# Seven-product projections in the scan of both layers, decays scaled on GpSimd, token sums kept

## The chip, the cores and the metric

The kernel runs on one core of one Trainium2 chip. Its time is the device time of one execution in microseconds. It is one launch that computes both blocks of the reference.

## The reference, cut to what matters

The first block is an attention block with a feed-forward part. The second block has two layers on 512 tokens: 256 latent tokens and 256 context tokens. The change sits in its layers, in the part that prepares and runs the state-space scan:

```python
def ssd_inputs(xbc_raw, dtf_raw, dtb_raw, conv_w, conv_b, dt_bias_f, dt_bias_b):
    xbc = dwconv_silu(xbc_raw, conv_w, conv_b)          # 5 taps along the tokens, then silu
    xs, bm, cm = jnp.split(xbc, [...], axis=-1)         # x 2048 wide, B and C 8 groups x 128
    ...
# ssd_chunked, chunks of 128 tokens, forward and backward
xc = x * dt
cs = cumsum(dt * a)
chunk_states = einsum('bclgn,bclgr,bclgrp->bcgrpn', bc, exp(cs[:, :, -1:] - cs), xc)
lmat = exp(where(lower, seg, -inf))                     # seg: differences of cs inside a chunk
y = einsum('bclsg,bclsgr,bcsgrp->bclgrp', cb, lmat, xc) + einsum(..., cc, h_in, exp(cs))
# ssd_output
rmsnorm((yf + yb + ssd_d * xs) * silu(z), ssd_norm_g) @ w_ssd_o
```

`xbc_raw`, `z`, the time steps and the attention inputs are all slices of one product, `h @ w_in`, with `h` 512 tokens x 1024 in fp32. Layer 0 returns both token sets. Layer 1 returns the latent tokens only, so C and z are needed for 256 tokens there and x and B for 512.

## The kernel before

All activations stay in SBUF, features on the partitions and tokens along the free dimension. Weights come as tiles of 1024 x 128 (512 KB) through a ring of 10 slots, `W`, in the order of a list (`weight_tiles`). SyncE issues each load when its slot is free. The engines run from orders that are written out by hand, with semaphores between them.

**The scan.** It runs over 8 groups `g`. A group has six projection tiles: x0, x1, B, C, z0, z1. `front(g, t)` on TensorE makes one, as 8 matmuls over the contraction, each 512 tokens wide in layer 0; the trace shows an fp32 matmul as two instructions. The tiles of group g+1 are made between the steps of group g. TensorE's group is: `turned` (transposes of B, the C by B products, transposes of x), the states of three steps, the outputs of the chunks (4 in layer 0, 2 in layer 1), and the tiles of g+1 in between. Each raw tile lies in a PSUM bank. ScalarE's `center` multiplies it by the middle tap into `xs`, VectorE's `conv` adds the other four taps (L2409, `in0` from PSUM), ScalarE's `activated` applies silu.

**The decays.** GpSimd broadcasts the rows of cumulated sums from DRAM (`broadcast`). ScalarE computes differences and exponentials into `mt` (`below`, `raised`). VectorE's `masked` multiplies each of 8 128x128 blocks of a chunk by its time step and by the masked C by B product (L2445), and adds both directions (L2449). `decayed` makes the scaled x (L2422), `carried` the carried state (L2434, L2438). GpSimd multiplies the exponentials `ec` by C (L754: 6 instructions per group in layer 0, 4 in layer 1) and adds up squares for the norm (L765, two per group).

**Seven products.** Later stages (merge0, wout20, f10, f20, all in layer 0) already use a form with seven products for two tiles: with the contraction halved, the two output tiles and the two token halves, eight block products become seven. One such *unit* is `quick(j)`: 7 times 4 matmuls of 256 tokens into the banks A, D, C, B. GpSimd makes four weight sums of 128x512 (L781, L783, L784, L786), into two further slots of the ring. VectorE makes the token sums (`tokens_summed`, four instructions of 128x1024, or three when the same tokens are summed again). ScalarE copies the first part out of PSUM (`first_kept`), and VectorE's `combined` makes the results from it with five more instructions, one input always in PSUM (256, 256, 512, 256 and 512 columns, L2610 to L2624).

## Time and profile before

| what | value |
|---|---|
| median of 3 runs | 2700.45 us (2700.17 to 2704.59) |
| the profiled execution, its own time | 2700.33 us |
| its span | 2698.5 us |
| TensorE busy | 2669.2 us (99%) |
| VectorE busy | 1292.7 us (48%) |
| ScalarE busy | 761.9 us (28%) |
| GpSimd busy | 622.5 us (23%) |

The span goes from the first to the last instruction of the profiled execution; 1.8 us of its time lie around it. Shares are means over stages with different limits, so the rows below are taken stage by stage. Every row of a timeline gives the start, the duration, the engine and the line of the code; rows of one line that follow each other without a gap are merged, with their number behind the x.

### The profile page before, as it was taken

Reading aid. Unit: us, or ns where it says so; the run is one execution under the profiler, and the core shown is the slowest. Engines: PE = TensorE matmul, PEld = TensorE weight load, DVE = VectorE, ACT = ScalarE, POOL = GpSimd, SP = SyncE. Lnnn points to the kernel's source line nnn. Section 1 sums busy time; section 2 is a strip of 40 time slices with the busy share of each in tenths; the row PEclk is TensorE's granted clock in tenths of the full one; section 3 lists DMA queues with packets and bytes.
Section 4 is the critical chain, followed back from the end, with each engine's and each line's share of the span. In section 5 each row is a group of like instructions: output and inputs, shape, how many; then the busy total and the mean of one; then the engine's idle time right before and its main releaser. Section 6 shows DMA issues by size and latency. Waiting matters only on the chain.

```text
span 2698.5 us, 33892 instructions
## 1 busy us (share of the span) xinstructions
PE 2669.2 (99%) x13090; PEld 1984.5 (74%) x13090; DVE 1292.7 (48%) x2279; ACT 761.9 (28%) x1740; POOL 622.5 (23%) x534
## 2 busy tenths in 40 slices
PE   8999999999999999999999999999999999999999
PEld 6778885555555666788778888866666777888887
DVE  1432234778778334787668451146677523212101
ACT  2430002656656333100022110015545422101100
POOL 4000000223323122275424454403122122000000
PEclk9999999999999999999999999999999999999999
DMA  9356666434342221233355432264344222567552
GB/s 264 96 160 194 187 194 171 106 103 110 91 111 66 55 55 39 63 110 103 100 160 184 142 92 87 86 168 126 104 115 111 79 71 65 155 188 210 153 151 78
DMA packets 518992, 330.62 MB, mean 123 GB/s; under 512 B 15296, under 2 KB 485680, under 8 KB 518832
## 3 DMA queue, kind: packets, MB, share of 16 engines
q1 hardware_dynamic: 507600, 296.10, 38.7%
q0 software_dynamic: 10784, 31.46, 4.7%
q8 instruction: 105, 1.72, 0.3%
q10 hardware_dynamic: 448, 0.89, 0.1%
q14 instruction: 55, 0.45, 0.1%
HBM read 327.06 MB, written 1.34 MB: 122 GB/s over the span
## 4 chain that ended last, share of the span: by engine, by line
PE 93%; DVE 2%; issue 2%; ACT 1%; PEld 1%; POOL 0%; DMA 0%; DVEq 0%; PEldq 0%; POOLq 0%; ACTq 0%
PE ps L1266 43%; PE ps L1646 23%; PE ps L1802 4%; PE ps L1814 3%; PE ps L1793 3%; PE ps L1955 3%; PE ps L1777 2%; PE ps L1916 1%; PE ps L1754 1%; PE ps L1939 1%; PE ps L1587 1%; PE ps L1928 1%; PE ps L2032 1%; PE ps L1292 0%; PE ps L1740 0%
## 5 line engine op out<-in xcount | busy, mean ns | idle before, releaser
L1266 PE MATMUL ps<-xnT,W 128*128 128x256 f32 (+1 forms) x2912 | 901.3, 468 | 2.2 <-DVE TMP L2409 0.9
L1266 PEld LDWEIGHTS ps<-xnT,W 128*128 128x128 f32 x2912 | 549.6, 190 | 320.0 <-issue 257.9
L1266 PE MATMUL ps<-BIG,W 128*128 128x256 f32 x1440 | 315.0, 379 | 0.0
L1266 PEld LDWEIGHTS ps<-BIG,W 128*128 128x128 f32 x1440 | 272.6, 190 | 37.1 <-issue 0.4
L1646 PE MATMUL ps<-TMP,W 128*128 128x256 f32 x1192 | 273.3, 379 | 0.0
L1646 PEld LDWEIGHTS ps<-TMP,W 128*128 128x128 f32 x1192 | 226.5, 190 | 30.8
L1646 PE MATMUL ps<-BIG,W 128*128 128x256 f32 x1016 | 230.5, 379 | 0.0
L803 ACT ACTIVATE TMP<-ps 128x512 f32<-128x512 f32 (+5 forms) x172 | 89.5, 528 | 440.9 <-PE ps L1646 209.6
L1646 PEld LDWEIGHTS ps<-BIG,W 128*128 128x128 f32 x1016 | 192.8, 190 | 27.1 <-issue 1.0
L2409 DVE SCALAR_TENSOR_TENSOR TMP<-ps,prmT,TMP 128x510 f32<-128x510 f32 (+3 forms) x256 | 181.6, 714 | 42.6 <-ACT TMP L1002 27.8
L2445 DVE SCALAR_TENSOR_TENSOR TMP<-TMP 128x128 f32<-128x128 f32 x384 | 162.4, 494 | 41.6 <-ACT TMP L1038 41.6
L1646 PE MATMUL ps<-xnT,W 128*128 128x256 f32 x704 | 161.0, 380 | 0.0
L781 POOL TENSOR_TENSOR W<-W 128x512 f32<-128x512 f32 x52 | 72.6, 1396 | 366.7 <-PE ps L1646 224.6
L754 POOL TENSOR_TENSOR BIG<-BIG,TMP 128x512 f32<-128x512 f32 x80 | 104.0, 1315 | 227.2 <-ACT BIG L1044 227.2
L1646 PEld LDWEIGHTS ps<-xnT,W 128*128 128x128 f32 x704 | 133.4, 190 | 18.6 <-DVE TMP L2624 0.4
L2140 DVE SCALAR_TENSOR_TENSOR TMP<-W,cact,TMP 128x512 f32<-128x512 f32 x168 | 142.4, 882 | 8.0
L730 POOL TENSOR_TENSOR TMP<-TMP,cst 32x512 f32<-32x512 f32 x56 | 71.6, 1279 | 274.6 <-ACT TMP L803 272.1
L1814 PE MATMUL ps<-W,xnT 128*128 128x128 f32 x1024 | 123.0, 276 | 0.0
L1814 PEld LDWEIGHTS ps<-W,xnT 128*128 128x128 f32 x1024 | 118.2, 192 | 3.8 <-issue 3.8
L1802 PE MATMUL ps<-xnT,W 128*128 128x512 f32 x256 | 119.0, 599 | 0.0
L832 ACT ACTIVATE xnT<-hT 128x512 f32<-128x512 f32 (+1 forms) x48 | 24.7, 522 | 333.8 <-DVE hT L2366 154.4
L1028 ACT ACTIVATE TMP<-BIG,TMP 128x128 f32<-128x128 f32 x384 | 116.8, 389 | 1.5 <-PE ps L1777 1.5
(350 smaller groups left out, 3002.5 us busy)
## 6 DMA issues: line engine op xcount, KB each, us to landing
W<-in_w_in SPq DMA_DIRECT2D x188, 512.0 KB, 4.0
W<-in_w_mlp SPq DMA_DIRECT2D x128, 512.0 KB, 4.0
W<-in_ada_w SPq DMA_DIRECT2D x96, 512.0 KB, 4.0
BIG<-cs_rows POOLq DMA_DIRECT2D x96, 256.0 KB, 4.7
W<-in_w_ssd_o SPq DMA_DIRECT2D x32, 512.0 KB, 3.6
W<-in_w_gate SPq DMA_DIRECT2D x22, 512.0 KB, 5.1
W<-in_w_up SPq DMA_DIRECT2D x22, 512.0 KB, 3.9
W<-in_w_down SPq DMA_DIRECT2D x16, 512.0 KB, 3.8
```

The costliest lines, as they stand in the source:

```text
L754: nc.gpsimd.tensor_tensor(e, e, xs[:, 3, ch * P:(ch + 1) * P].unsqueeze(1) .to_broadcast([P, 4, P]), ALU.mult).then_inc(ssd["ec"], 1)
L803: return A(dst, src, ACT.Copy)
L1028: last = A(mt[:, (2 * c + d) % 4, h, :], csb[:, ch, d, h, :], ACT.Relu, scale=-1.0, bias=tabs[:, 2, ch, span(g * 4 + 32 * d + h, 1)])
L1266: last = mm(dst, w[:, c, 0:m], rhs(k), start=k == 0, stop=k == total - 1)
L1646: done = mm(PS[bank][:, half * S:half * S + S], w[:, at + c, :], x[:, c, :], start=first and opens and c == 0, stop=last and closes and c ...
L1793: last = mm(PS[bq][:, 0:nt], w[:, c, :], xnT[:, c, 0:nt], start=c == 0, stop=c == KC - 1)
L1802: last = mm(PS[bk][:, :], w[:, c, :], xnT[:, c, :], start=c == 0, stop=c == KC - 1)
L1814: last = mm(PS[bq if h else 5][:, t * P:(t + 1) * P], xnT[:, c, t * P:(t + 1) * P], w[:, c, :], start=c == 0, stop=c == KC - 1)
L1955: last = mm(PS[4 + 2 * (i % 2) + n][:, 0:nt], w[:, c, :], xn(c), start=c == 0, stop=c == KC - 1)
L2140: last = V.scalar_tensor_tensor(out=dst, in0=w[:, k, :], scalar=c, in1=dst, op0=ALU.mult, op1=ALU.add)
L2409: last = V.scalar_tensor_tensor(out=acc[:, :, lo:hi], in0=raw[:, :, lo + k - 2:hi + k - 2], scalar=tap(l, g, t, k), in1=acc[:, :, lo:hi], ...
L2445: V.scalar_tensor_tensor(out=mt[:, c % 4, h, :], in0=mt[:, c % 4, h, :], scalar=tabs[:, 0, order[i], span(g * 4 + 32 * d + h, 1)], in1=cbm ...
```

## The change

- **Scan projections as units.** In layer 0 each group's (x0, x1), (B, C) and (z0, z1) become units of seven products, 24 in all. In layer 1 only (x0, x1) do, 8 in all. All use the banks 0, 1, 4, 5, so each unit waits, bank by bank, for `combined` of the unit before it. Their weight sums go to GpSimd inside the scan, and take two ring slots each.
- **Raw tiles in SBUF.** `combined` puts the raw tiles into `yz` or `zs`; `center`, `conv` and `gated` read them there and not in PSUM.
- **Decays.** GpSimd's `by_dt` multiplies `mt` by the time steps (one 128x512 instruction per chunk and direction). VectorE's `masked` becomes one instruction of 128x1024 and one of 128x512.
- **Scaled x.** VectorE copies all transposed x out of PSUM first (`xc`), and `decayed` reads that copy in SBUF.
- **Kept token sums.** The sums of the normed tokens get a place of their own (`TX`), are made once at the start of each scan and of f10, and serve the gate units of merge0 as well.
- **Order.** The time-step tile goes first in each scan, then the x unit. In layer 0, `masked(g, 1)` stands ahead of the convolutions, `masked(g, 2)` behind the first two, and two decay steps of the next group are moved up on ScalarE. One broadcast per chunk takes the place of two. The scratch for DMA descriptors is 8192.

```diff
+PARTS = {"x0": ("x0", "x1"), "bc0": ("B", "C"), "z0": ("z0", "z1"), "x1": ("x0", "x1")}
+QUICK = [(x, g, 0) for g in range(NG) for x in ("x0", "bc0", "z0")]
...
+    ph, n, _ = QUICK[FIRST_OF[g]]
+    if ph in PARTS:
+        return [0, 1, 4, 5]
...
+                def weights_summed(j):
+
+                    *pair, k1, k2 = quick_keys(j)
+                    wa, wb, w1, w2 = (slot_of(key) for key in (*pair, k1, k2))
+                    for key in pair:
+                        pool.wait_ge(slot_full[number[key] % SLOTS], full_at[number[key]])
+                    for key in (k1, k2):
+                        pool.wait_ge(slot_used[number[key] % SLOTS], number[key] // SLOTS)
+                    nc.gpsimd.tensor_tensor(w1[:, 0:4, :], wb[:, 0:4, :], wb[:, 4:8, :], ALU.add)
+                    pool.drain()
+                    nc.gpsimd.tensor_tensor(wb[:, 0:4, :], wa[:, 0:4, :], wb[:, 0:4, :], ALU.subtract)
+                    nc.gpsimd.tensor_tensor(w1[:, 4:8, :], w1[:, 0:4, :], wa[:, 0:4, :], ALU.subtract)
+                    pool.drain()
+                    nc.gpsimd.tensor_tensor(w2[:, 0:4, :], wa[:, 4:8, :], w1[:, 4:8, :], ALU.subtract).then_inc(q_s, 1)
+
+                def by_dt(g, i):
+
+                    ch = order[i]
                     for d in range(2):
-                        pool.dma_start(csb[:, ch, d, :, :], bass.AP(
-                            tensor=cs_dram, offset=(g * 4 + 32 * d) * T + ch * P, ap=[[0, P], [T, 4], [1, P]]))\
-                            .then_inc(csb_in[ch], 16)
-
+                        c = 2 * (n_ch * g + i) + d
+                        R("mexp", c + 1)
+                        m = mt[:, c % 4, :, :]
+                        nc.gpsimd.tensor_tensor(m, m, tabs[:, 0, ch, span(g * 4 + 32 * d, 4)].unsqueeze(2)
+                                                .to_broadcast([P, 4, P]), ALU.mult).then_inc(ssd["mdt"], 1)
+
...
                 for g in range(NG):
                     for i, ch in enumerate(order):
+                        by_dt(g, i)
...
                         if g < NG - 1:
                             broadcast(g + 1, i)
+                        if l == 0 and i == 1 and g < NG - 1:
+                            weights_summed(unit("bc0", g + 1))
+                            weights_summed(unit("z0", g + 1))
+                    if g < NG - 2:
+                        weights_summed(unit(f"x{l}", g + 2))
...
                 def center(g, t):
-                    made(act, ("ssd", l, g, FRONT[t]))
+                    if not is_quick(l, t):
+                        made(act, ("ssd", l, g, FRONT[t]))
                     if g:
                         R("tr", 3 * g)
                         if t < 2:
@@ -999,7 +1080,8 @@
                         if t == 3:
                             R("ec", len(parts) * g)
                     n = wide_of(t)
...
+                    if l == 0:
+                        if g == 0:
+                            decays(0, 0)
+                            below(0, 1)
+                        raised(g, 1)
...
+                if ph in PARTS:
+                    pe.wait_ge(dt_dve, 9 * int(ph[-1]) + 1)
+                    pe.wait_ge(ssd["xc"], ssd_first["xc"] * int(ph[-1]) + n)
...
+                def front(g, t):
+                    if t < 4:
+                        pe.wait_ge(q_rel, 3 * quick_group(unit("x1", g)) + 1)
+                    else:
...
-                front(0, 0, shifted("f20" if l else "down1"))
+                ready = shifted("f20" if l else "down1")
...
-                front(0, 2)
+                quick(unit(f"x{l}", 0))
+                if l == 0:
+                    after = quick_steps(unit("bc0", 0))
+                    for _ in range(3):
+                        next(after)
+                else:
+                    front(0, 2)
                 pe.wait_ge(dt_dve, 9 * l + 3)
...
-                        front(g + 1, 0)
+                        x_unit = quick_steps(unit(f"x{l}", g + 1))
+                        for _ in range(4):
+                            next(x_unit)
...
+                    if more and l == 0:
+                        quick(unit("bc0", g + 1))
...
-                    raw = PS[t % 2][:, 0:n].rearrange("p (s n) -> p s n", n=S)
+                    raw = (kept_tile(l, g, t) if is_quick(l, t) else PS[t % 2][:, 0:n]).rearrange("p (s n) -> p s n", n=S)
...
-                                               PS[4 + ch // 2][:, (ch % 2) * S:(ch % 2) * S + S]
-                                               .rearrange("p (h e) -> p h e", e=HD), per_head(1, ch, d, g), ALU.mult)
+                                               xc[:, ch, :].rearrange("p (h e) -> p h e", e=HD),
+                                               per_head(1, ch, d, g), ALU.mult)
...
                 def masked(g, i):
-                    for d in range(2):
-                        c = 2 * (n_ch * g + i) + d
-                        R("mexp", c + 1)
-                        for h in range(4):
-                            V.scalar_tensor_tensor(out=mt[:, c % 4, h, :], in0=mt[:, c % 4, h, :],
-                                                   scalar=tabs[:, 0, order[i], span(g * 4 + 32 * d + h, 1)],
-                                                   in1=cbm[:, d, order[i], :], op0=ALU.mult, op1=ALU.mult)
-                    dve.drain()
-                    V.tensor_tensor(mt[:, (c - 1) % 4, :, :], mt[:, (c - 1) % 4, :, :], mt[:, c % 4, :, :], ALU.add)\
-                        .then_inc(ssd["mready"], 1)
+                    c = 2 * (n_ch * g + i)
+                    m = mt[:, c % 4:c % 4 + 2, :, :]
+                    R("mdt", c + 2)
+                    V.tensor_tensor(m, m, cbm[:, :, order[i], :].unsqueeze(2).to_broadcast([P, 2, 4, P]), ALU.mult)
+                    dve.drain()
+                    V.tensor_tensor(m[:, 0, :, :], m[:, 0, :, :], m[:, 1, :, :], ALU.add).then_inc(ssd["mready"], 1)
...
-                conv(0, 0)
+                dve.wait_ge(n_sh, 8 * NORMS["f20" if l else "down1"])
+                all_summed(sums_job(unit(f"x{l}", 0)))
...
                 adds(*GAP["f20" if l else "down1"])
+                combined(unit(f"x{l}", 0))
+                conv(0, 0)
                 conv(0, 1)
-                conv(0, 2)
+                if l == 0:
+                    combined(unit("bc0", 0))
+                else:
...
-                    R("tr", 3 * g + 2)
+                    R("tr", 3 * g + 3)
+                    if g:
+                        R("ychunk", n_ch * g)
+                    for b in range(2):
+                        last = V.tensor_copy(flat(xc[:, 2 * b:2 * b + 2, :]), PS[4 + b][:, :])
+                    last.then_inc(ssd["xc"], 1)
                     dve.drain()
                     cb = PS[7][:, 0:nt].rearrange("p (c t) -> p c t", t=P)
                     for d, tri in enumerate((upper, lower)):
                         last = V.tensor_tensor(cbm[:, d, 0:n_ch, :], cb, tri.unsqueeze(1).to_broadcast([P, n_ch, P]), ALU.mult)
                     last.then_inc(ssd["cbm"], 1)
-                    R("tr", 3 * g + 3)
                     if g:
                         R("states", 3 * g)
                     decayed(g, 0)
                     decayed(g, 1)
-                    if g:
-                        R("ychunk", n_ch * g)
-                    for b in range(n_ch // 2):
-                        last = V.tensor_copy(flat(xc[:, 2 * b:2 * b + 2, :]), PS[4 + b][:, :])
-                    last.then_inc(ssd["xc"], 1)
                     R("cbm", g + 1)
                     masked(g, 0)
                     carried(g, 0)
                     decayed(g, 2)
+                    if l == 0:
+                        masked(g, 1)
                     if more:
+                        combined(unit(f"x{l}", g + 1))
+                    dve.drain()
+                    carried(g, 1)
+                    if l and more:
+                        masked(g, 1)
                         conv(g + 1, 0)
-                    elif l == 0:
+                    dve.drain()
+                    carried(g, 2)
+                    if l and not more:
                         masked(g, 1)
-                    dve.drain()
-                    carried(g, 1)
                     if more:
-                        masked(g, 1)
+                        if l == 0:
+                            conv(g + 1, 0)
                         conv(g + 1, 1)
-                    dve.drain()
-                    carried(g, 2)
                     if l == 0:
                         masked(g, 2)
+                        if more:
+                            combined(unit("bc0", g + 1))
                         masked(g, 3)
-                    elif not more:
-                        masked(g, 1)
                     if more:
...
+                    if more and l == 0:
+                        combined(unit("z0", g + 1))
```
## Rows read from the trace of the kernel before

**Rows 1.** Page, parts 1 and 4: busy time by engine, and the chain by engine.

```profile
PE 2669.2 (99%) x13090; PEld 1984.5 (74%) x13090; DVE 1292.7 (48%) x2279; ACT 761.9 (28%) x1740; POOL 622.5 (23%) x534
...
PE 93%; DVE 2%; issue 2%; ACT 1%; PEld 1%; POOL 0%; DMA 0%; DVEq 0%; PEldq 0%; POOLq 0%; ACTq 0%
```

**Rows 2.** Windows: one group of layer 0, one of layer 1, then the two openings.

```profile
core 0: us, PE busy (x) PEld busy (x) DVE busy (x) ACT busy (x) POOL busy (x), PEclk, DMA share, GB/s
...
627.53:678.88 51.35, 51.33 (x210) 26.76 (x209) 38.59 (x73) 32.32 (x67) 16.32 (x16) 1.00 0.39 103
...
1908.77:1947.15 38.38, 38.38 (x173) 24.61 (x172) 26.71 (x54) 19.72 (x43) 9.45 (x10) 1.00 0.41 110
423.60:473.93 50.33, 50.06 (x180) 24.75 (x177) 26.96 (x51) 16.27 (x32) 6.51 (x9) 1.00 0.64 165
1791.21:1832.00 40.79, 39.91 (x178) 24.49 (x175) 25.98 (x52) 15.28 (x31) 3.58 (x5) 1.00 0.62 161
```

**Rows 3.** Timeline, TensorE, layer 0 (start, us): transposes of two groups, one pair of tiles.

```profile
576.18 0.60 PE L1729 MATMUL ps<-cst,TMP 128*128 128x128 f32 x4
...
603.96 13.90 PE L1266 MATMUL ps<-xnT,W 128*128 128x512 f32 x32
...
627.53 0.60 PE L1729 MATMUL ps<-cst,TMP 128*128 128x128 f32 x4
```

**Rows 4.** Timeline, TensorE, stage f10: one seven-product unit and the start of the next.

```profile
1443.39 3.62 PE L1646 MATMUL ps<-TMP,W 128*128 128x256 f32 x16
...
1455.47 3.62 PE L1646 MATMUL ps<-TMP,W 128*128 128x256 f32 x16
```

**Rows 5.** Timeline, VectorE, layer 0, two groups of the scan.

```profile
604.16 0.76 DVE L2434 TENSOR_TENSOR TMP<-TMP 128x256 f32<-128x256 f32 x2 [2.58 <-PE ps L1754]
...
611.63 4.21 DVE L2445 SCALAR_TENSOR_TENSOR TMP<-TMP 128x128 f32<-128x128 f32 x8
...
616.52 6.33 DVE L2409 SCALAR_TENSOR_TENSOR TMP<-ps,prmT,TMP 128x508 f32<-128x508 f32 x8
...
624.11 1.29 DVE L2562 TENSOR_TENSOR BIG<-BIG 128x512 f32<-128x512 f32 x2
...
646.86 2.19 DVE L2445 SCALAR_TENSOR_TENSOR TMP<-TMP 128x128 f32<-128x128 f32 x8
```

**Rows 6.** Timeline, GpSimd, same stretch.

```profile
612.23 2.67 POOL L754 TENSOR_TENSOR BIG<-BIG,TMP 128x512 f32<-128x512 f32 x2 [0.23 <-ACT BIG L1044]
```

**Rows 7.** Timeline, GpSimd and VectorE side by side, stage merge0.

```profile
1299.87 1.22 DVE L2577 TENSOR_TENSOR TMP<-BIG,TMP 128x1024 f32<-128x1024 f32 x1
...
1303.75 1.27 POOL L783 TENSOR_TENSOR W<-W 128x512 f32<-128x512 f32 x1
...
1304.98 2.25 POOL L784 TENSOR_TENSOR W<-W 128x512 f32<-128x512 f32 x1
1306.19 2.11 DVE L2575 TENSOR_TENSOR TMP<-BIG,TMP 128x1024 f32<-128x1024 f32 x1
...
1307.37 2.06 POOL L786 TENSOR_TENSOR W<-W 128x512 f32<-128x512 f32 x1
1308.23 2.29 DVE L2577 TENSOR_TENSOR TMP<-BIG,TMP 128x1024 f32<-128x1024 f32 x1
```

**Rows 8.** One line each: ns shortest/median/longest; carried state, last part of a unit, GpSimd over hT.

```profile
L2434 DVE TENSOR_TENSOR TMP<-TMP x64: 418/424/1483, 489.4 to 2115.0; 128x256 f32<-128x256 f32 x64
...
L2624 DVE TENSOR_TENSOR TMP<-TMP,ps x32: 686/687/689, 1152.4 to 1782.7; 128x512 f32<-128x512 f32 x32
...
L795 POOL TENSOR_TENSOR hT<-hT,prmT x1: 3603/3603/3603, 1170.0 to 1170.0; 128x2048 f32<-128x2048 f32 x1
```

**Rows 9.** Timeline, VectorE, first and last step of the time-step chain, layer 0.

```profile
434.63 0.47 DVE L2469 TENSOR_SCALAR BIG<-ps,small 128x256 f32<-128x256 f32 x1
...
444.46 0.35 DVE L2493 TENSOR_SCALAR BIG<-BIG,small 128x256 f32<-128x256 f32 x1
```

**Rows 10.** Windows, TensorE clock just ahead of stage f10.

```profile
1378.00:1388.00 10.00, 9.77 (x59) 5.33 (x62) 3.54 (x9) 1.92 (x4) 0.00 (x0) 0.83 0.99 299
```

428 lines of the change are left out of this document (246 added, 182 removed).

## The prediction

> **What bounds the kernel now.** I read the page first: TensorE is busy 99% of the span, and 93% of the chain that ended last is TensorE [rows 1]. VectorE and GpSimd look half empty, but those are means over the whole span. So I went on to the windows of the stretches that the change touches. One group of layer 0's scan takes 51.35 us, with TensorE busy all of it and VectorE for 38.6; one of layer 1 takes 38.38 us, VectorE 26.7 [rows 2]. The starts of two `turned` give the same 51.35 us [rows 3]. The reader is to see that TensorE sets the scan today, and that VectorE has only 12.8 us a group to spare in layer 0. Then I read VectorE and GpSimd side by side, since the change loads both.
>
> **What TensorE saves.** A pair of 512-wide tiles takes 13.90 us in 32 instructions [rows 3]. A unit takes 12.08 us (1455.47 - 1443.39) [rows 4]: 1.8 us less. Three units a group leave TensorE 51.35 - 3 x 1.8 = 45.95 us in layer 0, and one leaves 38.38 - 1.8 = 36.6 us in layer 1. With 32 units, 58 us would go if TensorE stayed the bound everywhere.
>
> **What VectorE and GpSimd do to each other.** Near 1305 us both work on SBUF alone. A VectorE instruction of 1024 columns takes 1.22 us by itself and 2.11 and 2.29 us beside GpSimd; a GpSimd one of 512 columns takes 1.27 us by itself and 2.25 and 2.06 beside VectorE [rows 7]. They take turns. The carried state, 256 columns, takes 0.42 us, but 1.48 once [rows 8]. Eight of L2445 take 2.19 us alone and 4.21 us while two of GpSimd run (2.67 us) [rows 5, 6]: nearly the sum. A part of a unit with one input in PSUM never waits: shortest 686 ns, longest 689 [rows 8]. So each time a GpSimd instruction meets a VectorE one with two SBUF inputs, VectorE loses 2.11 - 1.22 = 0.89 to 1.07 us for a full one; I take 0.85, since `by_dt` is shorter (below).
>
> The Trainium skill says the same in "SBUF — State Buffer", section "Who interferes with whom": the pair of ports is an exclusive lock, held for the whole instruction, and a VectorE instruction with two SBUF inputs contends with a GpSimd one that reads SBUF. The trace agrees on who contends, but its price is 0.2 to 0.4 us under a whole instruction of 1.27. By the skill's wording the group of layer 0 would last at least the sum of both engines' such instructions, 33.6 + 25.2 = 58.8 us as an estimate, and the kernel 2752 us.
>
> **What the change puts on that path, layer 0, one group.** GpSimd: 12 weight sums, 6 `ec`, 2 sums of squares at 1.27 us, and 8 `by_dt`. For `by_dt` the nearest row has its broadcast along the inner axis as well: 3.60 us for 2048 columns [rows 8], so about 1.0 us for 512; 1.27 is the other end. Sum 20 x 1.27 + 8 x 1.03 = 33.6 us, before 8 instructions and 16.3 us with the broadcasts [rows 2]. One broadcast takes the place of two per chunk, which gives GpSimd back 3 us of issue; it lies beside other work.
>
> VectorE: the copies of x 1.28 and the masked products 1.28 (pairs of 512 columns, as [rows 5]); `decayed` 6 x 0.33 = 2.0; `masked` 4 x (1.22 + 0.08 + 0.61) = 7.7, before 4 x (2.2 to 4.2, + 0.7); carried state 0.6 + 2 x 1.45 = 3.5; the convolutions 16 x 0.80 = 12.9 (616.52: 6.33 for 8); three `combined` at 2.7 = 8.1, from 0.69 and 0.41 us rows and their gaps; the gated output 2.55. Sum 39.3 us. So `masked` gives back what `combined` costs. That is without meetings. What is new is where inputs lie: `conv` (16) and `decayed` (6) read PSUM before and SBUF now. With `masked` (8), `carried` (4) and the output (2), 36 instructions can meet GpSimd's 28.
>
> How many do? I followed both orders by hand from the last transpose of a group. GpSimd's two sums of squares run under VectorE's PSUM copies, two or so under each of `combined` x and `combined` bc, and one or two under the carried additions. GpSimd then waits for the squares of the next group, so it can't spread its work. That leaves 19 meetings: 16.2 us. VectorE then needs 39.3 + 16.2 + 1.1 (waiting for the last transposes, since those wait for z's `combined`) = 56.6 us. A second way to the same number: the third `masked` ends after 22.9 us of VectorE's own work and 17 meetings, at 37.4 us; `outputs(g, 2)` on TensorE waits for it, from about 30 us on, when bc is done; behind it are queued the z unit and the next group's `turned`: 1.5 + 6.9 + 1.4 + 5.2 + 0.7 + 0.9 = 16.6, in all 54.0 us. VectorE's own order is the later one. I take 56.6 us, 5.25 more than now. Seven groups (the last projects nothing): +36.8 us. Break-even is 51.35, or 13 meetings.
>
> **Layer 1.** GpSimd gets 4 `by_dt` and 4 weight sums, VectorE 27.5 us of own work, with convolutions of x alone from SBUF. The chain to the last convolution of the next group: 28.9 us with the wait for the first exponentials, about 6 meetings (5), silu 0.5 and `turned` 1.8 = 36.2, against TensorE's 36.6. Two limits as close as this seldom both hold: I take 37.5 us, between 36.6 and 38.4. Seven groups: -6.2 us.
>
> **The openings.** Layer 0's takes 50.3 us now, layer 1's 40.8 [rows 2]. TensorE saves 5.4 and 1.8 in them. But VectorE first makes four token sums (4.9 us) and then the time-step chain, 434.63 to 444.81 = 10.2 us [rows 9], and only then `combined` of the first x unit. The next unit needs its bank 0, which that `combined` frees. By hand TensorE is done with x at 443 and gets the bank at 450 in layer 0, 7 us of waiting; the first `turned` comes at 477.5, not 473.9: +3.6. Layer 1, where GpSimd is quiet: 2.7 us of waiting and later convolutions, +2.3. If this cover fails more, the price is up to VectorE's 15 us.
>
> The kept token sums take VectorE work out of merge0, where TensorE is the bound: 0. GpSimd's sums in f10 and the order of f10's token sums: 0, hidden by TensorE's units. More slots in the ring: the loads have 12 of 10 slots a group in a longer group; f10 lives with the same pattern at 12.08 us a unit [rows 4]; 0.
>
> **Sum.** 2700.3 (the profiled execution's own time; the median is 2700.45) + 36.8 + 3.6 - 6.2 + 2.3 = 2736.8: **2737 us**, slower by 1.3%. From the bounds of the meetings: 17 and 22 of them give 2725 and 2755.
>
> **Rivals.**
> - *TensorE stays the bound* (the other side). It needs VectorE's waits under 45.95 - 39.3 - 1.1 = 5.5 us a group, 6 meetings. 2700.3 - 37.8 - 12.6 + 5.9 = 2656 us. For it: VectorE's own sum fits. Against it: GpSimd runs 34 of 46 us, and nearly every overlap is paid [rows 5 to 7].
> - *The work interleaves as well as it can.* Held times alone (GpSimd 29.8 us at 1.13 and 0.9, VectorE 18.7 at one column a cycle of its 1024 in 1.07) make 48.5 + 1.1 = 49.6 us a group: 2688 us. Against it: GpSimd's wait for the squares.
> - *TensorE's clock falls too.* After the forecast's 7 to 9 us of waiting in each group the granted clock may drop to 1.2 GHz; it stood at 0.83 over 10 us in the thin work ahead of f10 [rows 10], 3.4 us at the lower level. Once a group on the path, 1.7 us x 7: 2749 us; with more meetings up to 2770.
>
> **Chances.** Forecast 0.50 (own range 2712 to 2760), TensorE bound 0.15, good interleaving 0.15, clock 0.15, worse 0.05. The range leaves out the first rival and the worst: 2684 to 2770. A measurement here can tell 0.2%, 5.4 us. Faster: the first rival and most of the second, 0.26; same 0.06; slower 0.68.
>
> **What would show it.** In the windows a group of layer 0 near 56 us, with VectorE near or over 50 busy and TensorE not full; L2409's successor over 0.75 us on average with a longest near 1.8; L2434's median well over 0.42; TensorE waiting at the third `outputs` for `masked`. In layer 1 a group of 36.6 to 38.4. In the openings a TensorE wait ahead of the second unit. It is wrong if groups of layer 0 take 46 us: then the meetings were few, or their price was paid by GpSimd alone, whose work has slack.

## The result, and the profile after

The changed kernel takes 2885.97 us (median of 4 runs, 2885.05 to 2887.91), the one before 2700.31 (4 runs): ratio 1.0686, interval 1.0668 to 1.0705. The forecast was 2737. The direction was right, the size 5 times too small: +185.7 us in place of +36.5. The profiled execution took 2885.49 us, its span 2883.7.

The page after, parts 1 and 4, against [rows 1]:

```profile
PE 2670.3 (93%) x13858; PEld 2160.5 (75%) x13858; DVE 1517.1 (53%) x2109; ACT 755.6 (26%) x1758; POOL 907.5 (31%) x712
...
PE 71%; DVE 15%; DVEq 6%; issue 3%; ACT 2%; POOL 1%; PEld 1%; DMA 0%; POOLq 0%; PEldq 0%; ACTq 0%
```

TensorE is as long busy as before, though it has less to do, and VectorE now holds 21% of the chain that ended last. The windows of one group of layer 0, one of layer 1 and the two openings, against [rows 2]:

```profile
core 0: us, PE busy (x) PEld busy (x) DVE busy (x) ACT busy (x) POOL busy (x), PEclk, DMA share, GB/s
746.03:810.75 64.72, 49.23 (x282) 42.35 (x281) 59.69 (x60) 30.57 (x68) 41.26 (x32) 0.89 0.32 82
2044.42:2093.53 49.11, 40.19 (x197) 31.37 (x196) 36.46 (x46) 20.49 (x44) 19.88 (x16) 0.93 0.33 86
423.60:485.78 62.18, 51.28 (x258) 40.12 (x258) 49.23 (x71) 17.84 (x36) 24.86 (x19) 0.93 0.33 89
1897.53:1946.12 48.59, 41.99 (x202) 30.13 (x199) 32.71 (x60) 15.25 (x31) 7.68 (x8) 0.93 0.40 105
```

This group of layer 0 takes 64.7 us where it was 51.35, this one of layer 1 takes 49.1 where it was 38.4 (48.1 on average over seven groups), and in none of the four stretches is TensorE busy throughout any more. TensorE's timeline at the end of the layer 0 group shows where it stands (in brackets the idle time and who ended it), the first row of `turned` being the last here:

```profile
778.37 1.89 PE L1748 MATMUL ps<-xnT,W 128*128 128x256 f32 x8
793.03 0.69 PE L1885 MATMUL ps<-TMP 128*64 128x128 f32 x4 [12.78 <-DVE TMP L2636]
...
795.79 4.83 PE L1748 MATMUL ps<-xnT,W 128*128 128x256 f32 x16
800.45 3.62 PE L1748 MATMUL ps<-TX,W 128*128 128x256 f32 x16
...
810.75 0.60 PE L1839 MATMUL ps<-cst,TMP 128*128 128x128 f32 x4
```

It waits 12.8 us for the third masked product, as the prediction's second way had it, and of the z unit that follows the outputs the first 16 matmuls take 4.83 us, the next 16 take 3.62. What was not foreseen is on VectorE. Its timeline, and GpSimd's for the same microseconds:

```profile
751.02 4.58 DVE L2612 TENSOR_TENSOR TMP<-TMP 128x256 f32<-128x256 f32 x4
755.52 5.59 DVE L2634 TENSOR_TENSOR TMP<-TMP 128x1024 f32<-128x1024 f32 x1
```

```profile
753.87 1.45 POOL L821 TENSOR_TENSOR BIG<-BIG,TMP 128x512 f32<-128x512 f32 x1
755.26 0.92 POOL L774 DMA_DIRECT2D BIG<-cs_rows  x1
756.20 2.04 POOL L800 TENSOR_TENSOR TMP<-TMP 128x512 f32<-128x512 f32 x2
758.19 1.27 POOL L821 TENSOR_TENSOR BIG<-BIG,TMP 128x512 f32<-128x512 f32 x1
759.40 0.92 POOL L774 DMA_DIRECT2D BIG<-cs_rows  x1
```

One `masked` of 1024 columns, 1.21 us by itself, takes 5.59. Before 755 us the two engines take turns. Then GpSimd issues a broadcast (L774) and behind it, without a pause, two `by_dt`, one `ec` and the next broadcast; all three run at their own speed (1.02, 1.02 and 1.27 us), and VectorE gets through only with the next DMA issue. I count the waits of VectorE as the duration of each instruction whose inputs all lie in SBUF, less the shortest of its kind, where that is over 0.1 us. From the first to the eighth `turned` of layer 0 that is 154.8 us, 63.1 of them in 13 such long waits (each 3.5 us or more); in layer 1 72.5 us, 32.7 in 7. Before it was 35.8 and 14.4, none long.

The whole difference, by the starts of `turned` (first one; seven groups of layer 0; to the first of layer 1; seven groups of layer 1; the rest): +12.0, +92.9, +9.1, +67.4, +3.6 = 185.0 us. The third also holds the opening of layer 1. Forecast were +3.6, +36.8, +2.3, -6.2 and 0.

### The profile page after: what moved, and what is told of

Read it like the earlier page. It is cut to its first block, busy times and chain, and to the rows that moved or that the text cites. A ratio compares the mean times of both kernels' runs of the same rounds, so it can differ in the third digit from the quotient of the medians.

```text
span 2883.7 us, 35791 instructions
## 1 busy us (share of the span) xinstructions
PE 2670.3 (93%) x13858; PEld 2160.5 (75%) x13858; DVE 1517.1 (53%) x2109; ACT 755.6 (26%) x1758; POOL 907.5 (31%) x712
## 3 DMA queue, kind: packets, MB, share of 16 engines
q1 hardware_dynamic: 507600, 296.10, 36.6%
## 4 chain that ended last, share of the span: by engine, by line
PE 71%; DVE 15%; DVEq 6%; issue 3%; ACT 2%; POOL 1%; PEld 1%; DMA 0%; POOLq 0%; PEldq 0%; ACTq 0%
PE ps L1748 26%; PE ps L1364 23%; DVE TMP L2599 6%; PE ps L1909 3%; PE ps L1920 3%; PE ps L2084 3%; PE ps L1900 2%; DVE TMP L2634 2%; DVEq L2603 2%; DVE TMP L2612 1%; DVEq L2567 1%; PE ps L2045 1%; DVEq L2635 1%; PE ps L1885 1%; PE ps L2068 1%
## 5 line engine op out<-in xcount | busy, mean ns | idle before, releaser
L1364 PE MATMUL ps<-xnT,W 128*128 128x256 f32 (+1 forms) x1888 | 465.6, 408 | 25.8 <-DVE TMP L2599 22.9
L1364 PEld LDWEIGHTS ps<-xnT,W 128*128 128x128 f32 x1888 | 367.3, 196 | 121.6 <-issue 44.8
L1748 PE MATMUL ps<-TX,W 128*128 128x256 f32 x1696 | 383.7, 383 | 10.6 <-issue 4.0
L1748 PEld LDWEIGHTS ps<-TX,W 128*128 128x128 f32 x1696 | 324.3, 192 | 57.5 <-issue 9.5
L786 POOL TENSOR_TENSOR W<-W 128x512 f32<-128x512 f32 x84 | 121.6, 1448 | 758.0 <-DMA W<-in_w_in 395.1
L1748 PE MATMUL ps<-xnT,W 128*128 128x256 f32 x1304 | 306.0, 387 | 7.2 <-DVE BIG L2565 7.2
L1748 PEld LDWEIGHTS ps<-xnT,W 128*128 128x128 f32 x1304 | 250.9, 194 | 44.7 <-DVE BIG L2565 7.6
L2599 DVE SCALAR_TENSOR_TENSOR TMP<-BIG,prmT,TMP 128x508 f32<-128x508 f32 x192 | 224.3, 1175 | 26.1 <-ACT TMP L1083 14.3
L1748 PE MATMUL ps<-TMP,W 128*128 128x256 f32 x688 | 157.6, 379 | 0.0
L788 POOL TENSOR_TENSOR W<-W 128x512 f32<-128x512 f32 x84 | 117.0, 1393 | 106.1 <-issue 97.3
L1885 PE MATMUL ps<-TMP 128*64 128x128 f32 x384 | 44.3, 308 | 111.3 <-DVE TMP L2636 105.3
L1748 PEld LDWEIGHTS ps<-TMP,W 128*128 128x128 f32 x688 | 130.7, 190 | 17.8
L791 POOL TENSOR_TENSOR W<-W 128x512 f32<-128x512 f32 x84 | 129.1, 1537 | 12.2 <-issue 0.4
L789 POOL TENSOR_TENSOR W<-W 128x512 f32<-128x512 f32 x84 | 132.9, 1582 | 0.0
```

The lines of the kernel that those rows point to most:

```text
L786: nc.gpsimd.tensor_tensor(w1[:, 0:4, :], wb[:, 0:4, :], wb[:, 4:8, :], ALU.add)
L788: nc.gpsimd.tensor_tensor(wb[:, 0:4, :], wa[:, 0:4, :], wb[:, 0:4, :], ALU.subtract)
L789: nc.gpsimd.tensor_tensor(w1[:, 4:8, :], w1[:, 0:4, :], wa[:, 0:4, :], ALU.subtract)
L791: nc.gpsimd.tensor_tensor(w2[:, 0:4, :], wa[:, 4:8, :], w1[:, 4:8, :], ALU.subtract).then_inc(q_s, 1)
L1364: last = mm(dst, w[:, c, 0:m], rhs(k), start=k == 0, stop=k == total - 1)
L1748: done = mm(PS[bank][:, half * S:half * S + S], w[:, at + c, :], x[:, c, :], start=first and opens and c == 0, stop=last and closes and c ...
```

## The experiments

All of these are edits of the changed kernel unless it is said otherwise, three rounds each, `d1`, `e1` and `e2` five. The table has each run's median and, from its profiled execution, the same five stretches.

| run | us | first `turned` | 7 groups, layer 0 | middle | 7 groups, layer 1 | rest |
|---|---|---|---|---|---|---|
| before | 2700.3 | 473.8 | 359.2 | 999.1 | 269.3 | 597.2 |
| after | 2886.0 | 485.8 | 452.1 | 1008.2 | 336.7 | 600.8 |
| a1 | 2828.3 | 491.0 | 426.9 | 1008.4 | 301.5 | 600.2 |
| a2 | 2837.5 | 485.2 | 435.5 | 1008.2 | 306.8 | 599.3 |
| a3 | 2919.3 | 484.5 | 489.0 | 1012.5 | 326.6 | 600.8 |
| a4 | 2838.6 | 486.4 | 444.0 | 1008.1 | 299.9 | 597.9 |
| b1 | 2834.1 | 486.7 | 435.0 | 1009.6 | 301.3 | 600.2 |
| b2 | 2825.7 | 489.4 | 425.0 | 1008.4 | 303.3 | 598.5 |
| b3 | 2758.4 | 476.2 | 382.5 | 1008.4 | 287.5 | 601.1 |
| b4 | 2750.2 | 474.1 | 408.6 | 1000.9 | 267.9 | 597.5 |
| c1 | 2813.5 | 486.4 | 410.3 | 1011.7 | 299.7 | 601.2 |
| c2 | 2740.9 | 474.6 | 365.1 | 1009.3 | 291.3 | 599.0 |
| c3 | 2774.9 | 486.2 | 394.9 | 1005.4 | 287.3 | 598.0 |
| c4 | 2699.4 | 480.9 | 336.4 | 1006.8 | 279.6 | 597.9 |
| d1 | 2696.6 | 479.9 | 353.6 | 1000.1 | 268.9 | 596.9 |
| d2 | 2688.9 | 483.7 | 336.5 | 1005.4 | 267.1 | 599.6 |
| d3 | 2816.5 | 489.3 | 409.9 | 1013.7 | 301.4 | 600.2 |
| e1 | 2691.9 | 474.1 | 348.9 | 1000.0 | 268.9 | 596.9 |
| e2 | 2691.2 | 474.0 | 349.3 | 1000.3 | 268.9 | 596.9 |

The first column also holds up to some 5 us, in `d2` more, by which some executions start late ahead of all that is changed (`d1`'s first tile of layer 0 starts at 428.7, not 423.6 [rows 2]).

**a1: who issues the broadcasts.**

```diff
-                        if g < NG - 1:
-                            broadcast(g + 1, i)                  # GpSimd
+                    if g < NG - 1:                               # ScalarE, end of raised(g, i)
+                        act.dma_start(csb[:, ch, ...], ...).then_inc(csb_in[ch], 16)
```

> The broadcasts of the cumulative sums are issued by ScalarE, right behind its own last exponential on that buffer, and no longer by GpSimd. All arithmetic stays. Theory 1: in the changed kernel a GpSimd instruction run that starts behind such a DMA issue shuts one VectorE instruction out until the next issue (13 waits of 5.6 to 6.1 us in layer 0, 7 of 5.4 in layer 1, 96 us in all). Without DMA issues on GpSimd no VectorE wait is over 2 us, each long wait becomes about three short turns (2.7 us); layer 0's groups fall from 64.8 to about 56 us, layer 1's from 49 to 45.5, the kernel from 2886 to about 2800. Rival, volume alone: the waits are the sum of what GpSimd holds, wherever the DMA is issued; long waits turn into as many short ones, groups stay at 63 to 65 and the kernel at 2870 to 2886.

Measured 2828.28 us, ratio 1.047 (1.0452 to 1.0487): 58 us back by moving an issue. The same place, VectorE and then GpSimd:

```profile
741.27 4.57 DVE L2618 TENSOR_TENSOR TMP<-TMP 128x256 f32<-128x256 f32 x4
745.77 2.06 DVE L2640 TENSOR_TENSOR TMP<-TMP 128x1024 f32<-128x1024 f32 x1
```

```profile
744.11 1.45 POOL L819 TENSOR_TENSOR BIG<-BIG,TMP 128x512 f32<-128x512 f32 x1
745.52 3.20 POOL L800 TENSOR_TENSOR TMP<-TMP 128x512 f32<-128x512 f32 x2
748.68 1.71 POOL L819 TENSOR_TENSOR BIG<-BIG,TMP 128x512 f32<-128x512 f32 x1
```

The `masked` that took 5.59 us takes 2.06, and `by_dt` now gives way. No wait in either layer is long; 149 short ones make 119.0 us in layer 0. The edit also takes the time of issuing off GpSimd, and idle time of GpSimd behind its issues (see the last section), so the 58 us are the worth of all three; no run separates them. But a group there takes 61 us, not the 56 that both this expectation and the prediction had.

**a3: a pause behind each issue.**

```diff
                             broadcast(g + 1, i)
+                            pool.wait_ge(csb_in[ch], 16 * (8 * l * (ch < 2) + g + 2))
```

> GpSimd still issues the broadcasts, but waits for each one to land before its next instruction (a pause of a few us, four a group in layer 0, two in layer 1). Theory 1: the run behind the issue is broken, the long waits vanish though the DMA and the arithmetic stay; layer 0's groups 56 to 59, layer 1's 45 to 47, 2800 to 2830 us. Rival, volume alone: nothing gained, GpSimd finishes later: 2886 to 2920.

2919.34 us (1.0793 to 1.0825). Both theories are half right. The long waits are gone though GpSimd still issues every DMA (115.3 us of waits in layer 0, all short), so a long wait takes the unbroken run behind the issue. The pause costs GpSimd more than that gave in layer 0 (70 us a group), and in layer 1, where it has time, 10 us are won.

**a2 and a4: the time steps back on VectorE**, alone and with `a1`'s edit.

```diff
-                        by_dt(g, i)
...
-                    V.tensor_tensor(m, m, cbm[...].to_broadcast([P, 2, 4, P]), ALU.mult)
+                        for h in range(4):
+                            V.scalar_tensor_tensor(out=mt[:, c % 4, h, :], in0=mt[:, c % 4, h, :],
+                                                   scalar=tabs[...], in1=cbm[...], op0=ALU.mult, op1=ALU.mult)
```

> One part undone: GpSimd no longer multiplies by the time steps, VectorE's masked does it again in eight instructions a chunk. Theory 1: behind a broadcast only one or two GpSimd instructions are left before the next, so the long waits shrink from 5.6 to about 1.3 to 2.5 us; that gives back 8 us a group in layer 0, and VectorE's own work takes back 6.3: 63 us a group, 48 in layer 1, 2865 us. Rival, volume alone: eight meetings fewer at 0.85 give back 6.8 of the 6.3 added: 64.3 us a group, 2880.

> Both edits together. Theory 1: no long waits; VectorE's own work in a layer 0 group 45.6 us, 12 GpSimd weight sums, 6 exponential products and 2 sums of squares left, about 13 meetings of 0.85: 58 us a group, 2 more than with ScalarE's issue alone, about 2815 us. Rival, volume alone: 64 us a group, 2875.

2837.52 and 2838.62 us. Undoing this part gives back 48 us by itself, more than I expected; in the trace of `a2` one long wait is left in place of 20. On top of `a1` it gives nothing: `a4` is 10 us slower than `a1`, and 24 over what was expected. Why `a4` loses 9 us to `a2` in layer 0 I did not settle.

**b1 and c1: the order on VectorE in layer 0**, on top of `a1`.

```diff
+                            masked(g, 2)                         # b1 and c1
+                            combined(unit("bc0", g + 1))         # c1 alone
                             conv(g + 1, 0)
                         conv(g + 1, 1)
                     if l == 0:
-                        masked(g, 2)
-                            combined(unit("bc0", g + 1))         # c1 alone
                         masked(g, 3)
```

> ScalarE issues the broadcasts (as in a1), and in layer 0 VectorE makes the third masked product ahead of the first two convolutions of the next group, not behind them. In a1 a group is 61.4 us: 40.9 from the last transposes to the third masked product, then 20.5 of TensorE (outputs, z unit, the next transposes). Theory 2: the order is the path, for TensorE stands 9.3 us at that product with 13 us of convolutions ahead of it. Then TensorE's wait goes and VectorE's own sum (54.6 busy and about 3 of gaps) is the bound: 57 to 58 us a group, about 2802. Rival: VectorE's total is already the bound: 61.4 stays, 2828.

> ScalarE issues the broadcasts, and in layer 0 VectorE makes both the third masked product and the combined tiles of bc ahead of the first two convolutions. In b1 the group stayed at 62 us since TensorE's next wait, 11 us for the combined tiles of bc, took the first one's place: VectorE's 43.6 us from the last transposes to there and TensorE's 17 us behind it stand in a row. Theory (two engines in a row, by the order of the work): the z unit starts at the end of the bc unit, 58 to 59 us a group with VectorE now the bound (56 busy and 2 to 3 of waits), about 2808. Rival (VectorE's total and the meetings are the bound already): 61 to 63 us, 2828 to 2840.

`b1` took 2834.11 us, 6 more than `a1`: nothing won. TensorE's waits in one group, `a1` and then `b1`, say why (engine, line, who is waited for: us, times, longest):

```profile
PE ps L1891 <- DVE TMP L2642: 11.9, 2, 9.3
```

```profile
PE ps L1754 <- DVE BIG L2571: 11.0, 1, 11.0
PE ps L1891 <- DVE TMP L2642: 2.5, 1, 2.5
```

The wait for `masked` had only hidden the next one, that of the z unit for the combined tiles of bc. With both moved, `c1` took 2813.49 us and 58.6 us a group, as expected: VectorE's stretch and TensorE's tail had stood in a row.

**b2 and d3: the order in layer 1**, both with ScalarE's issue.

```diff
-                        masked(g, 1)                             # b2; VectorE
                         conv(g + 1, 2)
+                        masked(g, 1)
-                        for _ in range(4):                       # b2; TensorE, parts of x ahead of states
+                        for _ in range(2 if l else 4):
-                        decays(g, 1)                             # d3, and c1's order; ScalarE
                         first_kept(unit(f"x{l}", g + 1))
+                        decays(g, 1)
```

Not shown of `b2`: VectorE's first masked product goes behind the first carried state, and z's first tile on TensorE ahead of the second chunk's outputs.

> ScalarE issues the broadcasts, and in layer 1 the order alone is changed: TensorE takes the first two states after two of the six parts of the x unit, z0 between the two outputs; VectorE takes the first masked product behind the first carried state and the second behind the convolution of B. In a1 a group of layer 1 is 44.2 us with 38.3 us of TensorE work; VectorE waits 3.6 us for GpSimd's by_dt and z0 waits 3.3 us for the convolution of B, with two z tiles (7 to 9 us) and the transposes behind it. Theory 2 (the chain masked, convolution of B, z, transposes sets the group, and not meetings): 39 to 41 us a group, 2828 - 7 x 4 = 2795 to 2805. Rival, the granted clock and the meetings set it: 43 to 44, 2820 to 2828.

> The whole change, output the reference's, with what helped: ScalarE issues the broadcasts, layer 0 in c1's order, layer 1 with that copy moved. Layer 0 as c1 (58.6 us a group), layer 1 from 43 to 41 if the order is the path there, 2813 - 14 = 2799; rival, the wait for by_dt (3.6 us) still sets layer 1: 2813.

2825.70 and 2816.54 us: layer 1 stays at 43 us a group; both times the rival was right. Neither of these two orders helps it so long as GpSimd's work is there.

**b3, c3 and c4: GpSimd's two new loads left out**, one at a time and both, on top of `a1`.

```diff
+                    if QUICK[j][0] in PARTS:                     # b3, c4, c2: no sums of weights
+                        pool.sem_inc(q_s, 1)
+                        return
...
-                        by_dt(g, i)                              # c3, c4: no time steps at all
-                    R("mdt", c + 2)
+                    R("mexp", c + 2)
```

> ScalarE issues the broadcasts, and GpSimd leaves out the sums of weights in the scans' projections (the units multiply by whatever lies in those slots; the output is not the reference's). GpSimd's work in a layer 0 group falls by 12 instructions of 1.27 us, in layer 1 by 4. By the prediction's price each meeting costs VectorE 0.85 us: 7 to 9 of them go, 6 to 8 us a group in layer 0 (61.4 to 54 or 55), 1 to 3 in layer 1 (44.2 to 42), and the opening of layer 0 shortens by up to 12: about 2760. Rival, by_dt and the exponential products make most of the meetings: 59 us a group and 2800 or more.

> ScalarE issues the broadcasts, and the multiplication by the time steps is left out altogether (output not the reference's); VectorE's masked stays at two instructions a chunk. Against a1 it prices by_dt: 8 GpSimd instructions fewer in a layer 0 group, 4 in layer 1, and no wait of masked for them (3.6 us a group in layer 1). By meetings at 0.8 us and TensorE's tail behind them: layer 0 from 61.4 to 54 or 55, layer 1 from 44.2 to 40 or 41, about 2755. Rival (by_dt is short and hidden): 60 and 44, 2820.

> ScalarE issues the broadcasts; the multiplication by the time steps and the sums of weights of the scans are both left out (output not the reference's). What is left of GpSimd is 6 exponential products and 2 sums of squares a group. It shows the change's schedule with hardly any meetings: by the prediction's first rival TensorE would be the bound, 46 us in layer 0 and 36.6 in layer 1, 2656 us. If the order of the work costs by itself, layer 1 stays over 38.4 (39 to 40) and layer 0 at 47 to 50: 2690 to 2710.

2758.41, 2774.86 and 2699.40 us. Against `a1` the sums of weights cost 69.9 us, the time steps 53.4, both 128.9. Windows of a group of layer 0, in the order `a1`, `b3`, `c3`, `c4`, each from its own trace:

```profile
736.30:797.70 61.40, 49.54 (x281) 42.60 (x280) 54.63 (x60) 30.90 (x68) 41.49 (x28) 0.92 0.32 86
```

```profile
694.90:749.50 54.60, 48.69 (x281) 42.18 (x280) 48.46 (x60) 30.86 (x68) 23.94 (x16) 0.94 0.37 97
```

```profile
656.70:713.60 56.90, 49.52 (x281) 42.61 (x280) 50.16 (x60) 30.91 (x68) 31.29 (x20) 0.91 0.37 93
```

```profile
673.30:721.30 48.00, 46.53 (x281) 40.41 (x280) 43.05 (x61) 30.79 (x68) 12.53 (x8) 1.00 0.44 110
```

VectorE does the same work each time (but for the window's edge); it is busy 54.6 us or 43.1 by what GpSimd does beside it. And only at 48.0 us does TensorE run at its full clock.

**c2: the units without GpSimd's two new loads**, VectorE with its old `masked`.

> The units alone, with GpSimd nearly quiet: ScalarE issues the broadcasts, VectorE multiplies by the time steps again, and the sums of weights are left out (output not the reference's). If meetings are all that the units cost, TensorE is the bound: 46 to 48 us a group in layer 0, 36.6 in layer 1, about 2660. If the late delivery of a unit's tiles costs by itself (both tiles of x come only with the end of the unit and three more additions, and all convolutions behind them), layer 1 stays at 40 to 41, and layer 0 at 52 or more: 2725 to 2745.

2740.92 us, 52.2 and 41.6 us a group, the second of the two cases. In layer 1 TensorE's waits fit a late delivery: 21.1 us in seven groups, all of z for the convolution of B. In layer 0 its 26.0 us of waits are for the third masked product, so there the units' additions and the old `masked` together on VectorE may be the cause; no run separates them.

**d2: one copy moved in `c4`**, the last edit of the diff of `d3` alone.

> c4 (ScalarE issues; no time steps, no sums of weights; output not the reference's) with one copy of ScalarE in layer 1 moved: the first product of the x unit is copied out of its bank ahead of the second chunk's decays, not behind them. In c4 layer 1 stays at 40.0 us a group with hardly a meeting: VectorE waits 2.3 us for that copy and later TensorE waits 2.1 us for the convolution of B ahead of z, and its next 32 matmuls take 8.9 in place of 7.2 us. Theory (order of the work, then the clock): both vanish, 36.6 to 37.5 us a group, 2699 - 17 to 24 = 2675 to 2682. Rival: the next link of the chain (masked's wait for the exponentials) takes the place, 39 to 40 us, 2692 to 2699.

2688.94 us, 10.5 less than `c4`: 38.1 us a group in layer 1 where `c4` has 40.0, between the expectation (36.6 to 37.5) and its rival (39 to 40). TensorE's row for the two tiles of z and the windows, of two groups of `c4` with the same instructions:

```profile
1975.40 7.17 PE L1372 MATMUL ps<-xnT,W 128*128 128x256 f32 x32 [2.33 <-DVE TMP L2607]
...
2014.15 8.86 PE L1372 MATMUL ps<-xnT,W 128*128 128x256 f32 x32 [2.05 <-DVE TMP L2607]
```

```profile
1943.40:1982.40 39.00, 36.66 (x197) 29.28 (x196) 27.21 (x46) 20.51 (x44) 7.51 (x6) 1.00 0.41 108
1982.40:2022.80 40.40, 38.35 (x197) 30.48 (x196) 27.20 (x46) 20.51 (x44) 7.51 (x6) 0.96 0.41 105
```

Both have a wait of 2 us for the convolution of B. Behind the second the clock granted was the lower for a while, and 1.7 us went. In `d2` the wait is 1.4 us and z takes 7.17.

**b4: the kernel before with `by_dt` alone.**

```diff
+                        by_dt(g, i)
-                        for h in range(4):
-                            V.scalar_tensor_tensor(... in1=cbm[:, d, order[i], :] ...)
+                    R("mdt", c + 2)
+                    V.tensor_tensor(m, m, cbm[:, :, order[i], :]..., ALU.mult)
```

> The kernel before with one part of the change alone: GpSimd multiplies by the time steps, VectorE's masked is two instructions; no units, two broadcasts a chunk issued by GpSimd as before. Theory: TensorE stays the bound with VectorE at about 32 us of own work and under 10 meetings in 51.35: 2696 to 2706. Whether a long VectorE wait appears here too shows if it needs the units' load: by theory 1 it appears wherever by_dt of the next chunk is ready when the issue ends, which is rare here since ScalarE's exponentials come late. Rival: the longer chain from the exponential over GpSimd to masked delays outputs: 2715 to 2740.

2750.23 us, 48 more than before with no unit in it, and all of it in layer 0's groups (+49.4 us); the rival was right. VectorE and GpSimd in one of its groups:

```profile
714.68 2.21 DVE L2455 TENSOR_TENSOR TMP<-TMP 128x1024 f32<-128x1024 f32 x1 [4.64 <-POOL TMP L752]
716.96 4.15 DVE L2457 TENSOR_TENSOR TMP<-TMP 128x512 f32<-128x512 f32 x1
```

```profile
715.75 1.52 POOL L741 DMA_DIRECT2D BIG<-cs_rows  x2
717.28 2.05 POOL L752 TENSOR_TENSOR TMP<-TMP 128x512 f32<-128x512 f32 x2
719.27 1.27 POOL L765 TENSOR_TENSOR BIG<-BIG,TMP 128x512 f32<-128x512 f32 x1
720.49 1.53 POOL L741 DMA_DIRECT2D BIG<-cs_rows  x2
```

Here too is a long wait, with the old pair of issues, so neither the units nor the single larger transfer is its cause. And `masked` now waits for GpSimd (10.8 us in this group) with the convolutions, which free TensorE's banks, queued behind it: over the seven groups TensorE waits 30.9 us for them, and did not before. The seven groups have seven long waits, 24.2 us; how much of the 49 each of the two makes is not separated.

**d1, e1 and e2: units where nothing waits for them.** The kernel before, with one unit a group in layer 0, z of groups 1 to 7.

```diff
+PARTS = {"z0": ("z0", "z1")}
+QUICK = [("z0", g, 0) for g in range(1, NG)]
...
+                            R("mready", n_ch * g + 2)            # GpSimd; not in e2
+                            weights_summed(unit("z0", g + 1))
...
+        return [1, 4, 0, 5]                                      # banks in d1
+        return [1, 4, 5, 0]                                      # in e1 and e2
```

`e1` and `e2` also move the four token sums from the head of layer 0's opening to its end.

> The kernel before, with one unit a group in layer 0 alone: z of groups 1 to 7, whose tiles no convolution waits for. Time steps stay on VectorE, broadcasts as before, layer 1 and the openings as before; GpSimd sums the unit's weights only after the second masked product is done, when it stood idle for 16 us before; B takes z0's old place on TensorE, its convolution comes ahead of the third state, C goes to a bank that is free since the copies of x; token sums kept, 4.9 us beside the first tile. By the findings so far (a unit saves TensorE 1.8 us, c4 gave 3.3 of 5.4 us a group with hardly any meetings; what costs is GpSimd's SBUF work beside VectorE's and tiles that come late): VectorE 41 us of own work and 2 to 4 of meetings in 49.6, TensorE the bound, 51.35 to 49.6 us a group, 2701 - 12 = 2688. Rival: one of VectorE's in-order waits becomes TensorE's (third or fourth masked product, C's convolution), with the clock's loss behind it: 51 to 53 us a group, 2700 to 2712.

> d1 with its two leftovers taken away: in d1's groups of 50.6 us TensorE waits 0.7 us ahead of the transposes of x for the unit's last addition, which frees their bank; here the unit's last product and C share bank 0 and the transposes' banks come free one addition sooner. And the four token sums (4.9 us) go from the head of the opening, where they cost 0.8 us, to the end of it, where VectorE stood idle for 9.9 us. TensorE alone then sets layer 0: 51.35 - 1.73 = 49.6 to 49.8 us a group, 2701 - 12 + 0 = 2689 to 2691. Rival: C's bank now waits for the first convolution, or the next x0 for the unit's last addition, and one of them costs what was gained: 2696.

> e1, but GpSimd makes the unit's four sums of weights straight behind the second broadcast and does not wait for VectorE's second masked product. If the place of GpSimd's work is what counts, its 5 us now fall on the third state and the second masked product: 4 to 7 meetings, 3 to 6 us of VectorE's waiting a group, of which TensorE's slack hides a part: 49.8 to 52 us a group, 2691 to 2705. If VectorE has room enough anyway (it is busy 41 of 50 us): same as e1.

2696.58, 2691.91 and 2691.17 us. `d1` missed its 2688, with 50.5 us a group; the other two came as expected. `e1` is at 0.996 of before (0.9948 to 0.9973), a small gain but clear of the noise, and beats both kernels. One group of it:

```profile
623.64:673.51 49.87, 49.87 (x234) 31.34 (x233) 41.20 (x78) 32.90 (x69) 21.39 (x21) 1.00 0.40 106
```

TensorE is busy all of it, 1.5 us less than before a group. `e2` shows that where VectorE has 8 us to spare the place of GpSimd's sums does not matter: VectorE waits 17.5 us more over the seven groups, and the groups are 0.06 us longer.

## Why the prediction was wrong, step by step

The profiled execution took 149 us more than the forecast. 56 of them are gone in that of `a1`; of its remaining 93, the groups of layer 0 hold 31, those of layer 1 38, and the openings, the stages between and the late start of that execution 24.

**What bounds the kernel: right.** TensorE, with 12.8 us of VectorE's time to spare.

**The price of a meeting: right.** 0.85 was taken; `a1` has 149 waits of 0.80 us in layer 0. Their number too: 21 a group for 19, 17.0 us for 16.2. The Trainium skill ("SBUF — State Buffer", section "Who interferes with whom") has the pair locked for a whole instruction of whichever engine started first. In `a1` no wait is over 1.08 us, under the 1.27 us of a GpSimd instruction, which does not speak against that; in the changed kernel a long wait spans three or four of them and part of a DMA issue, and there the measurement differs from the rule. `by_dt` was taken at 1.03 us, its median is 1.05. VectorE's own work was taken at 39.3 us with its gaps; `a1` has 54.63 - 17.0 = 37.6 busy.

**"They take turns": wrong behind a DMA issue.** This is the first step that failed, in the term of the meetings. The prediction counted one GpSimd instruction for each meeting, also behind the broadcasts. The longest durations of the convolution and of `decayed` over the whole kernel (ns, shortest/median/longest) stand against it:

```profile
L2599 DVE SCALAR_TENSOR_TENSOR TMP<-BIG,prmT,TMP x192: 733/750/6118, 464.6 to 2271.9; 128x508 f32<-128x508 f32 x96, 128x510 f32<-128x510 f32 x96
...
L2612 DVE TENSOR_TENSOR TMP<-TMP x96: 407/806/5409, 491.1 to 2295.8; 128x256 f32<-128x256 f32 x96
```

With what else moving the issue frees on GpSimd it cost 58 us (`a1`): 3.6 us a group in layer 0, 5.0 in layer 1. In layer 1 the locked-out instruction is a `decayed` that TensorE's third state needs:

```profile
2064.83 2.07 PE L1862 MATMUL ps<-TMP 128*128 128x256 f32 x4 [4.67 <-DVE TMP L2612]
```

TensorE waits 26.3 us for it in seven groups, and not at all in `a1`. Before, every issue was followed by a wait of GpSimd for ScalarE, the shortest 0.23 us, so the trace of before could not show it. The last section has more.

**The group of layer 0: the later of two ways, where they had to be one chain.** The prediction worked out VectorE's sum, 56.6 us, and a second way over the third `masked` and TensorE's tail, 37.4 + 16.6 = 54.0, and took the larger. `a1` follows the second way, with both parts longer: 738.66 to 779.53 is 40.9 us to that `masked`, 17.6 of waits in it where 14.5 were taken, and then 20.5. The rows of TensorE in `a1`, then in `c4`, whose clock stays up:

```profile
779.59 0.69 PE L1891 MATMUL ps<-TMP 128*64 128x128 f32 x4 [9.33 <-DVE TMP L2642]
...
782.35 5.22 PE L1754 MATMUL ps<-xnT,W 128*128 128x256 f32 x16
787.41 3.62 PE L1754 MATMUL ps<-TX,W 128*128 128x256 f32 x16
```

```profile
706.00 0.44 PE L1893 MATMUL ps<-TMP 128*64 128x128 f32 x4 [1.47 <-DVE TMP L2644]
...
707.46 3.72 PE L1756 MATMUL ps<-xnT,W 128*128 128x256 f32 x16
711.01 3.62 PE L1756 MATMUL ps<-TX,W 128*128 128x256 f32 x16
```

From the first start to the last in each, 7.8 us and 5.0. So the forecast's 16.6 us for the tail was nearly right (`c4`'s is 17.7 with its transposes), and 2.8 us of the lower clock were left out. The third rival had the mechanism, at 1.7 us a group: it was no rival but part of every case in which TensorE waits long. The order made this chain, `c1` shows it: 2.4 us a group back.

**Layer 1: the chain's end was put in the wrong place.** The prediction let the chain end at the last convolution, with silu and `turned` behind it: 36.2 us. But z's first tile takes the bank of B, and so waits for the convolution of B, and two tiles, 7.2 us and in the lower clock 8.9, stand behind it. The changed kernel's row:

```profile
2084.84 8.86 PE L1364 MATMUL ps<-xnT,W 128*128 128x256 f32 x32 [3.26 <-DVE TMP L2599]
```

With hardly a meeting left the group is at 40.0 us (`c4`), not 36.6, and 38.1 at best (`d2`). What holds it above 36.6 is, as I read it, that both x tiles come only with the unit's end and all the convolutions after them; no run tests that alone. The remaining 3 us up to `a1`'s 43.1 are `by_dt` (a wait of 3.6 us) and the sums of weights, which cost much the same: 41.0 and 41.1 without the one or the other.

**The opening of layer 0: right cause, wrong size.** 7 us of TensorE's waiting for bank 0 were forecast, and 7.17 measured. But both ends came 5 us later than forecast (448 and 455 us, for 443 and 450), so the match is luck in part:

```profile
446.19 1.89 PE L1748 MATMUL ps<-xnT,W 128*128 128x256 f32 x8
455.24 6.13 PE L1748 MATMUL ps<-xnT,W 128*128 128x256 f32 x16 [7.17 <-DVE BIG L2565]
```

VectorE's seven steps of the series took 7.04 us, not 3.42, and each token sum 2.1 to 2.3, not 1.23, beside GpSimd's first sums of weights, and the 16 matmuls behind the wait 6.1 us, not 3.6; and within the x unit TensorE had already waited 3.0 us for the time-step chain. I had given GpSimd's work in this stretch no meeting at all. Without the sums of weights (`b3`) the first `turned` stands at 476.2, near the forecast's 477.5. **That of layer 1:** +7.8 us for +2.3, a wait of 3.8 us of z for a convolution (the same step that failed in the groups), with 9.5 for 7.2 us of z behind it, and the time-step product in the lower clock at 5.88 for 3.67 us, since no full tile runs ahead of it now.

**`by_dt` beside other work: too cheap.** "So `masked` gives back what `combined` costs" counted instructions alone. In `b4` the part by itself costs 49 us: `masked` must wait for a third engine, 73.4 us in layer 0's seven groups, with VectorE's queue behind it, and the long waits are there too. In the changed kernel that wait is 3.2 us in layer 0 and 24.8 in layer 1; whether ScalarE's new order or VectorE's own lateness hides it in layer 0 is not shown. On top of `a1` the time steps are worth 53 us (`c3`).

**Rivals.** *TensorE stays the bound*: nearly, and only with GpSimd's new work gone, at 48.0 and 40.0 us, not 45.95 and 36.6 (`c4`: same time as before, with 6 us of VectorE's waits a group still in layer 0). *Good interleaving*, 49.6: no. *Clock*: true, and added to the rest.

## What to carry to other kernels

A saving on the engine that bounds the kernel is paid on the others: lay out one round of the loop as a single chain across engines, with the wait for each bank in it, before adding up each engine's work. An engine's sum says when it becomes the bound; it does not say how long two engines stand in a row. Look at what an engine does straight behind a DMA issue of its own, and give the faster form first to work that nobody waits for: one unit of three, where its tiles are needed last, won 10 us, and the whole change lost 186.
